# A second up product by seven half-size block products, sums of weights made in DRAM, and a reordered end of a down product

## The reference, cut to what matters

```python
def first_block(x, ...):
    ...
    h2 = _rmsnorm(x, norm2_w) * (1.0 + scale2) + shift2
    ffn = jnp.dot(jax.nn.silu(jnp.dot(h2, w_ffn_gate)) * jnp.dot(h2, w_ffn_up), w_ffn_down)
    x = x + gate2 * ffn
    return _rmsnorm(x, final_norm_w)

def second_block(x, ...):
    ...
        z = rms_norm(h, attn_norm[l]) @ w_in[l]
        ...
        h = h + jnp.concatenate([o_nsa, o_gla], axis=-1) @ w_out[l]
        u = causal_dwconv(rms_norm(h, ffn_norm[l]) @ w_up[l], conv_w[l], conv_b[l])
        gate, up = jnp.split(u, 2, axis=-1)
        h = h + (jax.nn.silu(gate) * up) @ w_down[l]
    return h
```

## Time and profile before

| | |
|---|---|
| median of three runs | 1520.23 us (1519.48 to 1520.29) |
| profiled execution | 1521.84 us, span 1520.0 us |
| mean granted clock of the tensor engine | 0.994 of full |
| tensor engine busy | 1488.0 us, 98% |
| VectorE busy | 1107.5 us, 73% |
| ScalarE busy | 710.9 us, 47% |
| HBM traffic | 177 GB/s over the span |

### The profile page before, as it was taken

One profiled execution on the slowest core, in us unless ns is written; L12 is line 12 of the kernel. 1 busy time (PEld: TensorE's weight loads), 2 busy tenths in 40 slices (PEclk: granted clock), 3 DMA queues, 4 the chain that ended last, 5 costly groups with the idle time before them and its releaser, 6 DMA issues.

```text
span 1520.0 us, 22717 instructions
## 1 busy us (share of the span) xinstructions
PE 1488.0 (98%) x9247; PEld 1248.8 (82%) x9247; DVE 1107.5 (73%) x1841; ACT 710.9 (47%) x1158; POOL 64.2 (4%) x93
## 2 busy tenths in 40 slices
PE   7999999999999999999999889999999999999999
PEld 5777888778877899999988777777788988888887
DVE  6669888875587698888789766787567456556885
ACT  4453334653221365455465553766525334434653
POOL 1000000000000011000000112200011000000000
PEclk9999999999999999999999989999999999999999
DMA  9423124358687678967357417850114232233473
GB/s 386 146 76 99 62 69 140 112 177 308 224 292 278 231 262 245 256 173 188 98 165 218 150 32 245 180 111 30 57 56 129 93 109 83 86 111 97 135 230 127
DMA packets 87025, 238.09 MB, mean 157 GB/s; under 512 B 12037, under 2 KB 12165, under 8 KB 85769
## 3 DMA queue, kind: packets, MB, share of 16 engines
q1 hardware_dynamic: 68312, 204.87, 39.5%
q0 software_dynamic: 18608, 31.77, 9.8%
HBM read 222.94 MB, written 45.35 MB: 177 GB/s over the span
## 4 chain that ended last, share of the span: by engine, by line
PE 85%; DVE 9%; ACT 2%; DMA 2%; issue 1%; POOL 0%; SPq 0%; DVEq 0%; ACTq 0%
PE bank L831 81%; PE bank L843 4%; DVE AR L2144 2%; DVE wl L2110 1%; DMA CST<-in_down 1%; DVE ACC L2107 1%; DVE Hl L2144 1%; ACT wh L1544 1%; DVE AR L2454 1%; DVE CST L2144 1%; DVE X L2144 0%; DVE G L2151 0%; DMA raw<-in_wst 0%; DMA X<-in_x 0%; DVE AR L2151 0%
## 5 line engine op out<-in xcount | busy, mean ns | idle before, releaser
L1544 ACT ACTIVATE wh<-raw 128x1024 fp32r<-128x1024 f32 (+1 forms) x248 | 259.0, 1046 | 335.4 <-PE bank L831 284.7
L2110 DVE TENSOR_TENSOR wl<-raw,wh 128x1024 fp32r<-128x1024 f32 (+1 forms) x248 | 297.2, 1208 | 96.9 <-ACT wh L1544 96.8
L831 PE MATMUL bank<-wh,Hh 128*128 128x512 f32 (+1 forms) x732 | 296.1, 405 | 1.5 <-DVE Hl L2144 0.7
L831 PE MATMUL bank<-wh,Hl 128*128 128x512 f32 (+1 forms) x732 | 283.9, 388 | 0.0
L831 PE MATMUL bank<-Hh,wh 128*128 128x256 f32 (+2 forms) x824 | 279.1, 339 | 4.6 <-DVE wl L2110 3.0
L831 PE MATMUL bank<-wl,Hh 128*128 128x512 f32 (+1 forms) x732 | 283.3, 387 | 0.0
L831 PE MATMUL bank<-Hl,wh 128*128 128x256 f32 (+2 forms) x824 | 277.1, 336 | 0.0
L831 PE MATMUL bank<-Hh,wl 128*128 128x256 f32 (+2 forms) x824 | 277.0, 336 | 0.0
L831 PEld LDWEIGHTS bank<-Hh,wh 128*128 128x128 f32 (+1 forms) x824 | 156.5, 190 | 22.4 <-DVE wl L2110 3.4
L831 PEld LDWEIGHTS bank<-Hl,wh 128*128 128x128 f32 (+1 forms) x824 | 156.5, 190 | 16.6 <-issue 0.5
L831 PEld LDWEIGHTS bank<-Hh,wl 128*128 128x128 f32 (+1 forms) x824 | 156.4, 190 | 16.5
(11 more groups left out here) (298 smaller groups left out, 2365.8 us busy)
## 6 DMA issues: line engine op xcount, KB each, us to landing
raw<-in_wst SPq DMA_DIRECT2D x212, 512.0 KB, 4.5
sums_dram<-in_down POOLq DMA_DIRECT2D x11, 2816.0 KB, 32.8
raw<-sums_dram SPq DMA_DIRECT2D x37, 512.0 KB, 4.1
raw<-in_down SPq DMA_DIRECT2D x25, 512.0 KB, 4.4
CST<-in_down SPq DMA_DIRECT2D x11, 1024.0 KB, 6.0
sums_dram<-CST SPq DMA_DIRECT2D x11, 1024.0 KB, 4.6
AR<-in_wst SPq DMA_DIRECT2D x8, 1024.0 KB, 10.5
CST<-in_wst SPq DMA_DIRECT2D x10, 512.0 KB, 6.5
```

The costliest lines, as they stand in the source:

```text
L831: return e.matmul(o, l, r, start=start, stop=stop, skip_group_check=True)
L1544: e.activation(HI[slot[i]][:, 0:width(i)], raw_of(i), ACT.Copy).then_inc(*w_hi.mark(i))
L2110: e.tensor_tensor(LO[slot[i]][:, 0:n], raw_of(i), HI[slot[i]][:, 0:n].bitcast(f32), SUB).then_inc(*w_lo.mark(i))
```

## The change

1. **Second up product.** Strips 1 to 10 of `2up` are made as the first block's are, by `up_steps` and `up_product` (168 matmuls of 256 columns for one strip in place of 96 of 512). Since the convolution comes between, the four quarters of a strip are written to buffers `ZG` and `ZU`: ScalarE copies four banks (`taken_out`), VectorE combines three (`left_rows`, `left_up_rows`, `right_up_rows`), and `tap`, `conv`, `gate` and `product` work on the buffers, one for each channel tile, placed one by one.
2. **Sums of its weights.** They are made in DRAM, in `up_sums_dram` (four sums of ten strips of 512 KB), by GpSimd's queue: four plain copies once the second chunk of qr is split, two accumulating transfers behind the retention's roots, and two more, one after the other, behind `fourth_term`. The stored stream is laid out so that each quarter lies in one piece (`storage`), with B12 as chunks that are stored but not loaded. SyncE's load of a T chunk waits for its sum (`s_up_sums`).
3. **Planner.** The two extra slots belong to the down products alone; `2up` may be loaded as far ahead as `up`; in a down product two high parts can be made in one tick after step 3. The second down product's splits of rows for the steps 0 to 8 are placed as steps of it and at the end of strip 10.
4. **End of the first down product.** VectorE's order becomes: upper rows 0, upper rows 1, last norm and scale of tile 0, lower rows 0 six ticks on, tile 1's; `lower_rows(1)` goes from step 43 to 46; tile 2's square, root and scale are placed one to two ticks earlier.

The diff, cut to these parts:

```diff
-    for j in range(11):
-        block(f"2up{j}", ("w_up_2", "w_up_2"), 8, [(256 * j, 256), (FF + 256 * j, 256)])
+    block("2up0", ("w_up_2", "w_up_2"), 8, [(0, 256), (FF, 256)])
+    quarters = {"B11": (0, 0), "B21": (0, 4), "B12": (FF, 0), "B22": (FF, 4)}
+    for j, z in up_steps():
+        c, k = quarters.get(z, (0, 0))
+        plan.append(("2up" + z, j, "w_up_2" if z in quarters else None, k, 4, [(c + 256 * j, 256)]))
...
+    plan += [("2upB12", j, "w_up_2", 0, 4, [(FF + 256 * j, 256)]) for j in range(1, 11)]
...
+    lie = [i for i, c in enumerate(chunks) if c[2] is not None and c[0] not in apart]
+    return lie + [i for z in apart for i, c in enumerate(chunks) if c[0] == z]
...
-                if name == "dn" and hi_at[k]:
+                if name == "dn" and len(hi_at[k]) > (what[0] > 3):
...
+        if k and name in SEVEN and ticks[k - 1][0] != name:
+            avail += [(NH + v, place[ticks[k - 1][0] + z, 10]) for v, z in enumerate(("T1", "T2"))]
...
-                if not avail or rank[at] > here + ahead + 3 * (name == "up"):
+                if not avail or rank[at] > here + ahead + 3 * (name in ("up", "2up")):
...
+        up_sums_dram = nc.dram_tensor("up_sums_dram", (4, 10, P, 1024), f32, kind="Internal").ap()
...
-        SPLITS = {"dn": {0: 2, 2: 3, **SPLIT_AT}, "2dn": SPLIT_AT}
+        SPLITS = {"dn": {0: 2, 2: 3, **SPLIT_AT}, "2dn": {0: 2, 1: 3, 5: 4, 6: 5, 7: 6, 8: 7, **{s: n for s, n in SPLIT_AT.items() if n > 7}}}
...
+                return 5 if j == 1 else 7 if (key, j) == ("2up", 2) else 3
+            return 4 if j == 1 else 6 if (key, j) == ("2up", 2) else j % 2
 
...
-                    w.after(3, root)
+                    w.after(1, root)
                 else:
                     root()
-                w.after((3, 4, 4, 4)[t], lambda: norm_root("n3", t, dve.of(("last", "x", t))))
...
+            def taken_out(j, z):
+                event, to = {"B11": ("p1", ZG[j % 2][:, :, 0:256]), "T1": ("q5", ZU[j % 2][:, :, 256:512]),
+                             "T2": ("u", ZU[j % 2][:, :, 0:256]), "T4": ("right gate", ZG[j % 2][:, :, 256:512])}[z]
+                on.wait_ge(*dense.of(("2up", z, j)))
+                if j > 2:
+                    on.wait_ge(*dve.of(("2up", "conv", 2 * j - 3 if z in ("B11", "T4") else 22 + 2 * j - 3)))
...
+            def tap(j, half, m):
+                ch = 22 * half + 2 * j + m
+                if j == 0:
+                    on.wait_ge(*dense.of(("2up", 0, m + 2 * half)))
+                    x = bank[up_bank(0, m + 2 * half)][:, :]
+                elif half:
+                    on.wait_ge(*dve.of(("2up", "c12", j)))
+                    on.wait_ge(*dve.of(("2up", "c22", j)))
+                    x = ZU[j % 2][:, m, :]
+                else:
+                    on.wait_ge(*dve.of(("2up", "c11", j)))
+                    on.wait_ge(*act.of(("2up", "right gate", j)))
+                    x = ZG[j % 2][:, m, :]
+                if j > 0:
+                    on.wait_ge(*dve.of(("2up", "act", 2 * j - 2 + m)))
+                e.activation(CV[2 * m + half], x, ACT.Identity, scale=cw[:, 2, ch:ch + 1], bias=W("cb", ch, 1)).then_inc(*act.mark(("2up", "tap", ch)))
...
+                    if z in ("B11", "T1", "T2"):
+                        w.after(1 if what == (10, "T2") else 2, lambda j=j, z=z: taken_out(j, z))
+                    if z == "T3" and not last:
+                        w.after(2, lambda j=j: w.after(1, lambda: tap(j, 1, 0)))
+                        w.after(3, lambda j=j: w.after(1, lambda: tap(j, 1, 1)))
+                    if z == "T4" and not last:
+                        w.after(2, lambda j=j: [taken_out(j, "T4"), tap(j, 0, 0)])
+                        w.after(3, lambda j=j: [tap(j, 0, 1), gate(j, 0)])
+                        w.after(4, lambda j=j: gate(j, 1))
+                    if z == "T3" and last:
+                        w.after(3, lambda: [tap(10, 1, 0), tap(10, 1, 1)])
+                    if z == "T4" and last:
+                        w.after(1, lambda: [taken_out(10, "T4"), tap(10, 0, 0), tap(10, 0, 1)])
+                        w.after(3, lambda: [gate(10, 0), gate(10, 1)])
+                if what in FIRST_LEFT:
+                    left_high("2dn", FIRST_LEFT[what])
...
-                w.after((3, 4, 4, 4)[t], last_norm)
-                w.after((6, 6, 7, 7)[t], lambda: norm_scale("n3", t))
+                w.after((3, 4, 3, 4)[t], last_norm)
+                w.after((6, 6, 5, 7)[t], lambda: norm_scale("n3", t))
...
-                if r:
-                    lower_rows(0)
...
-                if s == 43:
+                if s == 46:
...
                         w.after(3, lambda r=r: upper_rows(r))
-                        after_dn(r)
+                        if r:
+                            after_dn(0)
+                            w.after(6, lambda: lower_rows(0))
+                            after_dn(1)
...
+                    if z == "B21":
+                        w.after(2, lambda j=j: left_rows(j))
+                    if z == ("B22" if j < 3 else "T2"):
+                        w.after(3, lambda j=j: left_up_rows(j))
+                    if z == "T3":
+                        w.after(1 if last else 2, lambda j=j: right_up_rows(j))
+                        w.after(3, lambda j=j: conv(j, 1, 0))
+                        w.after(3 if last else 4, lambda j=j: conv(j, 1, 1))
+                    if z == "T4":
+                        w.after(2, lambda j=j: conv(j, 0, 0))
+                        w.after(2 if last else 3, lambda j=j: conv(j, 0, 1))
+                        w.after(3 if last else 4, lambda j=j: product(j, 0))
+                        w.after(3 if last else 4 if j == 9 else 6, lambda j=j: product(j, 1))
...
+            whole = {z: wst[o:o + 10 * P * 1024].rearrange("(j p n) -> j p n", j=10, p=P) for z in ("B11", "B12", "B21", "B22") for o in (offs[place["2up" + z, 1]],)}
+            on.wait_ge(*w_lo.of(place["qr", 1]))
+            for i, z in enumerate(("B12", "B22", "B12", "B21")):
+                e.dma_start(up_sums_dram[i], whole[z]).then_inc(s_up_copy, 16)
...
+            on.wait_ge(s_up_copy, 64)
+            e.dma_start(up_sums_dram[0], whole["B11"], accum_op=ADD, max_dma_last_dim=8192).then_inc(s_up_sums, 16)
+            e.dma_start(up_sums_dram[2], whole["B22"], accum_op=ADD, max_dma_last_dim=8192).then_inc(s_up_sums, 16)
...
+            on.wait_ge(s_up_sums, 32)
+            e.dma_start(up_sums_dram[1], up_sums_dram[0], accum_op=ADD, max_dma_last_dim=8192).then_inc(s_up_sums, 16)
+            on.wait_ge(s_up_sums, 48)
+            e.dma_start(up_sums_dram[3], up_sums_dram[1], accum_op=ADD, max_dma_last_dim=8192).then_inc(s_up_sums, 16)
...
+                if key[:-1] == "2upT":
+                    on.wait_ge(s_up_sums, {"1": 32, "3": 32, "2": 48, "4": 64}[key[-1]])
```

More of the change, by code:

```diff
@@ L323, in up @@
         ticks.extend((prefix, (0, a, c), place[f"{prefix}0", c], a > 0) for a in (0, 256) for c in range(4))
[L324 to L327, removed]
+        ticks.extend((prefix, (j, z), place[prefix + z, j], True) for j, z in up_steps())
     def seven(key):
@@ L412, in schedule @@
             else:
-                while avail and avail[0][0] >= NH and not (place["dn7", 0] <= at < place["2kv", 0] or at >= place["2up0", 0]):
+                while avail and avail[0][0] >= NH and not (place["dn7", 0] <= at < place["2kv", 0] or at >= place["2dn7", 0]):
                     avail.pop(0)
@@ L452, in program @@
     widths = [c[4] * sum(n for _, n in c[5]) for c in chunks]
-    offs = [0]
-    for c, n in zip(chunks, widths):
-        offs.append(offs[-1] + P * n * (c[2] is not None))
+    offs, end = {}, 0
+    for i in storage(chunks):
+        offs[i] = end
+        end += P * widths[i]
     ctx = ExitStack()
@@ new lines, in left_rows, with left_up_rows @@
+            def left_rows(j):
+                on.wait_ge(*dense.of(("2up", "B21", j)))
+                on.wait_ge(*act.of(("2up", "p1", j)))
+                x = ZG[j % 2][:, :, 0:256]
+                tt(x, x, two(bank[up_product_bank("2up", j, "B21")][:, :]), ADD, ("2up", "c11", j))
+            def left_up_rows(j):
+                on.wait_ge(*dense.of(("2up", "B22", j)))
+                on.wait_ge(*act.of(("2up", "u", j)))
+                x = ZU[j % 2][:, :, 0:256]
+                tt(x, two(bank[2][:, :]), x, SUB, ("2up", "c12", j))
@@ new lines, in right_up_rows, with conv @@
+            def right_up_rows(j):
+                on.wait_ge(*dense.of(("2up", "T3", j)))
+                on.wait_ge(*act.of(("2up", "q5", j)))
+                x = ZU[j % 2][:, :, 256:512]
+                tt(x, x, two(bank[up_product_bank("2up", j, "T3")][:, :]), SUB, ("2up", "c22", j))
+            def conv(j, half, m):
+                ch, y = 22 * half + 2 * j + m, CV[2 * m + half]
+                x = bank[up_bank(0, m + 2 * half)][:, :] if j == 0 else (ZG, ZU)[half][j % 2][:, m, :]
+                on.wait_ge(*act.of(("2up", "tap", ch)))
```

(6 more changed lines are left out.)

211 lines of the change are left out of this document (110 added, 101 removed).

## The result

The changed kernel takes 1580.56 us (median of four runs, 1571.63 to 1582.16) against 1519.86: 1.0389 times as long, 95% interval 1.0368 to 1.041. Forecast were 1497.7 us, with 1512 as the upper end. The profiled execution took 1582.16 us, span 1580.3.

A forecast was written before the change was run, and what follows sets the result against it. The prediction took the matmul engine, busy 1488.0 of 1520.0 us, as the bound. 1521.84 - 16.0 + 1.0 + 0.5 - 8.0 = 1499.3, or 1497.7 us against the median, which is 1.6 lower; range 1490 to 1512.

The forecast's parts named there:

- The transfers: Weights' sums made in DRAM by copies and accumulates: expected to cost 0, bounds 0 and +33 us.
- rival 2: Early copies take the engines from weight loads, one split late: +33, 1531 us; chance 7% full, 12% mild.
- mild case: Half of the early copies' full delay to weight loads: +13, 1511 us; chance 12%.
- they fit: Copies and accumulates fit the engines' free share, 71% in 56:125 and 57% in 242:345, till about 142 and 347.
- 2up: Second up product, strips 1 to 10: -16.0 us by 1680 half-size matmuls, plus 1.0 us for its start.
- rival 3: VectorE binds the new up product, over 20.16 us per strip; one more microsecond a strip gives 1508 us; chance 8%.
- 2dn's start: Start of the second down product, with the end of strip 10's VectorE work: +0.5 us, bounds 0 to 3.
- its prefetch of weights: At the second down product's start, prefetch covers some 15 us of VectorE work on three steps of 2.7 us.
- dn's end: First down product's end to early 2kv: reordering shortens halts and avoids the slow clock, -8.0 us, bounds 0 and 13.9.
- the layout with 5.4 us of halts: First down product's end laid out anew from 860.1: tile halts of 2.1, 0.6, about 2.0 and about 0.7 us remain.
- rival 1: Reordering the down product's end gives nothing, as VectorE and the norm chain set 2kv's start: 1505.7 us; chance 14%.
- no slow stretch: At the first down product's end, the remaining short halts were expected to bring no lower clock.

The follow-up runs named there:

- e2: The changed kernel with the four plain copies cut into pieces of at most 8192 bytes instead of 65536: 1542.0 us, ratio 1.0142.
- e4: The kernel before with the whole new end of the first down product alone, planner and order together: 1516.71 us, ratio 0.9976.
- e7: The kernel before with only the planner's change for the first down product, two high parts in a step after step 3: 1520.08 us, ratio 1.0006.
- e8: The kernel before with only the reordered queue at the first down product's end, planner as it was: 1515.88 us, ratio 0.9976.
- e9: The changed kernel with 8192-byte copies, first two accumulates earlier, gate and row splits moved, the planner's old rule for dn: 1510.43 us, ratio 0.9939.

## Why the prediction was wrong

The forecast was 82.9 us too low. By the stages: transfers 65.1, start of 2dn 11.7, end of dn 5.3, 2up 3.4, less 2.2 of scatter, 83.3 together.

**The transfers** (taken at 0, came to 65.1). Two steps failed. The first was to read room from the share that the engines have free. e2's engines are at 0.82, and full in kr itself, with no loss, the changed kernel's at 0.70 with 40.9 us: what counts is how long one load takes, against how often the stage needs one. The second was the evidence against rival 2, "beside the accumulates loads only doubled". Those accumulates come in pieces of 2048 bytes that take 0.18 us; the row said nothing of pieces of 65536. The rival had the right mechanism, place and sign, with 7% for its full form. Its size was off too: it took one load to be late until the copies were through; in fact each of the next three paid 16 to 27 us, and its +33 was +40.9, 4.6 of it the lower clock. (Half of 33 is 16.5, not the 13 of its mild case.) For the first two accumulates there was no rival at all, though the same row shows loads slowed by accumulates. Theirs are pieces of 8192 bytes, a load takes 6.8 us beside them, and in gr, which needs a load every 4.6 us, that is a loss by itself: +24.2. The step to take was the sentence "they fit" with the load's time in place of the share.

The rule cited from the Trainium skill ("DMA: Bandwidth & Descriptors", "Queues, rings and completion order") has the engines take turns by packets of, typically, 9 to 17 descriptors. The traces agree with the turns, and not with packets of that size for these two queues: a load did not wait for one packet, it waited for one piece at each of its eight. The prediction named that alternative ("were each piece a packet of its own, rival 2 follows"), and it is the one that the records show. Nor would the sum have been safe by the first reading: an engine has five of a copy's 80 pieces of 65536 bytes, at 3.05 us each some 15 us for each load (an estimate), and SyncE issues four loads in kr's 27.3 us.

**2up** (-15.0 with its start, came to -11.6). The pace is right: 1680 matmuls of 256 columns, 202.50 busy of 206.10 us. The pauses were to cost 1.0 and cost 3.6 (206.10 - 202.50): the snapshot of T2 behind the gate, which the prediction called the tightest and held to be half a microsecond early, is 1.45 us late, twice, in strips 2 and 3. VectorE in these strips is busy for 172.42 of 206.10 us, 84%, less than the 91% reckoned; rival 3 did not happen.

**2dn's start** (+0.5, came to +12.2). The step that failed is a cover that does not exist. "Some 15 us of VectorE work on three steps of 2.7 us" was correct and then covered by "its prefetch of weights". A prefetch can hide a late load, not a late low part, which VectorE makes itself. The work is there because the split rows' buffers hold the up product's own sums until its last blocks (`left_free`: B22, T3, T4 of strip 10), so splits that strip 10's time used to cover now fall into the first steps of 2dn. The halts of 2.79 and 4.90 us were both followed by the lower clock (0.65 from 1468 to 1472 us, 0.50 from 1477.9 to 1482), matmul starts some 0.43 us apart in the second.

**dn's end** (-8.0, came to -2.7). The halts sum to 8.5 us after and 9.5 in e4, 9.1 before; what was won is the clock (0.96 in the window from 922.66 and 1.00 in e4, where the earlier trace rows has 0.86 and 0.80). The step that failed is the layout with 5.4 us of halts. It got the first right, 2.1 forecast and 2.42 measured, and left out the weights of 2kv, whose high parts stand behind norms and turns on ScalarE and one of whose low parts stands behind a norm's scaling on VectorE. These are the waits of 2.41 and 2.62 us:

```profile
934.52 1.09 PE L858 MATMUL bank<-CST,AR 128*128 128x128 f32 x8 [2.42 <-DVE AR L2207]
...
943.92 0.50 PE L846 MATMUL bank<-wh,Hh 128*128 128x512 f32 x1 [0.68 <-DVE wl L2170]
948.01 0.50 PE L846 MATMUL bank<-wh,Hh 128*128 128x512 f32 x1 [2.41 <-DVE wl L2170]
957.29 0.80 PE L846 MATMUL bank<-wh,Hh 128*128 128x512 f32 x1 [2.62 <-DVE wl L2170]
```

For the change as a whole rival 1 (the halts only move) was the better account. The planner's half, which the prediction took for the cure of the first halt, gives nothing (e7 +0.5 us) and takes 1.1 us from the order's half when the two come together (e8 -3.9, e4 -2.8). The order by itself does shorten the halts, 9.1 to 6.6 us; why the planner's half undoes this was not taken apart. Nor does the prediction's "no slow stretch" hold below halts of 4 us: the one of 2.62 us was followed by a clock of 0.55 (957 to 959 us), while in e4 one of the same length was followed by 1.00.

The **idea of the change** stands: with the copies cut to 8192 bytes, the accumulates ahead of the retention's roots, a gate and two splits moved and the planner's rule of before, it takes 1510.4 us (e9), 0.9939 of before. There the up product gives 13.9 us and the order at dn's end about 4, and the start of 2dn still takes 8.0 back; no kernel reached the forecast of 1497.7.

## What to carry to other kernels

Price a background transfer by its piece: a load of n pieces per DMA engine takes n times (own piece + foreign piece), and this has to be held against the rate at which the stage asks for loads, not against the free share of the engines. Cut DRAM-to-DRAM copies to the size of the loads that they run beside; these contiguous ones came in pieces of 65536 bytes where nothing was said. And work that is moved onto an engine is hidden only if the engine has room in that very stretch: add its microseconds step by step before calling it covered, above all where two stages meet.

## What was not expected of the hardware

Two queues of one DMA engine alternate piece by piece at very unequal lengths: 0.16 us (median) against 3.05 us, 254 load pieces to 238 copy pieces from 65 to 115 us. An accumulating piece of 8192 bytes takes 0.63 us, a copying one 0.36; at 2048 bytes, 0.18. Cutting the copies from 65536 to 8192 bytes lengthened them little: their median from issue to landing is 49 us as against 43. And halts of the matmul engine of equal length can be followed by different clocks: 2.62 us by 0.55 in the changed kernel and by 1.00 in e4.
